# Routing stage reordered on TensorE, and the first expert's tokens gathered directly in turned form

## What is computed

```
x = x + mix @ w_out
h = rmsnorm(x, ln_ffn_g)
logits = h @ w_router + b_router
top_val, top_idx = lax.top_k(logits, 4)
probs = softmax(top_val)
for each expert e:                      # 32 of them, 3 matrices of 1024x1024 each
    xb = rows of h whose top_idx holds e
    g = min(xb @ w_gate[e] + b_gate[e], 7);  u = clip(xb @ w_up[e] + b_up[e], -7, 7)
    a = g * sigmoid(1.702 * g) * (u + 1)
    y[those rows] += probs * (a @ w_down[e] + b_down[e])
x = x + y;  return rmsnorm(x, ln_final_g)
```

## Time and profile before

| | |
|---|---|
| median of three runs | 1139.98 us (1139.12 to 1140.4) |
| span of the profiled execution, first to last instruction | 1137.4 us |
| around the span (median less span) | 2.6 us |
| TensorE busy | 1092.5 us, 96% of the span |
| ScalarE / VectorE busy | 200.9 / 316.3 us |
| DMA | 439.24 MB, mean 386 GB/s |

### The profile page before, as it was taken

One profiled execution on the slowest core, in us unless ns is written; L12 is line 12 of the kernel. 1 busy time (PEld: TensorE's weight loads), 2 busy tenths in 40 slices (PEclk: granted clock), 3 DMA queues, 4 the chain that ended last, 5 costly groups with the idle time before them and its releaser, 6 DMA issues.

```text
span 1137.4 us, 12484 instructions
## 1 busy us (share of the span) xinstructions
PE 1092.5 (96%) x5391; PEld 494.9 (44%) x5391; DVE 316.3 (28%) x686; ACT 200.9 (18%) x350; POOL 3.6 (0%) x11
## 2 busy tenths in 40 slices
PE   7999999999999999999999999999999999999996
PEld 6888889733343333333333333333333333333332
DVE  7566778421111111111111111111111111111121
ACT  5345556210000000000000000001110000000011
POOL 0000000000000000000000000000000000000000
PEclk9999999999999999999999999999999999999999
DMA  9854229999999999999999999999999999999996
GB/s 351 269 175 159 110 77 405 414 403 414 427 429 426 429 426 429 428 428 429 428 429 428 429 427 429 428 428 429 429 428 428 429 428 429 429 429 428 426 427 256
DMA packets 46280, 439.24 MB, mean 386 GB/s; under 512 B 4106, under 2 KB 5666, under 8 KB 20900
## 3 DMA queue, kind: packets, MB, share of 16 engines
q1 hardware_dynamic: 46084, 438.48, 92.5%
q10 hardware_dynamic: 160, 0.27, 0.1%
HBM read 437.68 MB, written 1.05 MB: 386 GB/s over the span
## 4 chain that ended last, share of the span: by engine, by line
PE 80%; DMA 15%; DVE 2%; ACT 2%; issue 1%; SPq 0%; POOL 0%; DVEq 0%; POOLq 0%
PE ps L1075 49%; PE ps L722 5%; PE ps L1099 4%; DMA attn<-in_w_gate_dram 4%; PE ps L1004 4%; DMA attn<-in_w_up_dram 4%; DMA pool<-in_w_up_dram 4%; DMA pool<-in_w_down_dram 3%; PE ps L752 2%; PE ps L802 2%; PE ps L760 2%; PE ps L1052 1%; ACT o_t L656 1%; PE ps L855 1%; PE ps L857 1%; PE ps L856 1%
## 5 line engine op out<-in xcount | busy, mean ns | idle before, releaser
L1075 PE MATMUL ps<-pool,o_t 128*64 128x512 f32 x2144 | 482.6, 597 | 16.9 <-ACT o_t L656 12.1
L1075 PEld LDWEIGHTS ps<-pool,o_t 128*64 128x64 f32 x2144 | 148.6, 137 | 307.0 <-issue 282.7
L1545 DVE TENSOR_SCALAR v_tok<-ps 128x512 f32<-128x512 f32 x32 | 22.1, 692 | 497.7 <-PE ps L1075 497.7
L656 ACT ACTIVATE o_t<-ps 128x512 f32<-128x512 f32 x32 | 19.1, 597 | 323.1 <-PE ps L722 323.1
L1075 PE MATMUL ps<-slot_gt,o_t 128*64 128x512 f32 x304 | 69.4, 598 | 5.4 <-ACT o_t L656 4.1
L1075 PE MATMUL ps<-slot_wv,o_t 128*64 128x512 f32 x304 | 69.4, 598 | 4.1 <-ACT o_t L656 4.1
L1075 PE MATMUL ps<-attn,o_t 128*64 128x512 f32 x320 | 72.2, 593 | 1.1 <-DMA attn<-in_w_gate_dram 0.9
L643 ACT ACTIVATE attn<-v_tok 128x512 f32<-128x512 f32 x32 | 20.2, 630 | 247.4 <-DVE v_tok L1545 247.4
L1099 PE MATMUL ps<-attn,o_t 64*128 64x512 f32 x256 | 63.6, 615 | 0.0
L1004 PE MATMUL ps<-xs,work 128*64 128x512 f32 x256 | 60.7, 593 | 0.0
L722 PEld LDWEIGHTS ps<-cst,work 128*128 128x128 f32 (+1 forms) x294 | 35.8, 170 | 54.8 <-issue 52.1
(11 more groups left out here) (195 smaller groups left out, 952.7 us busy)
## 6 DMA issues: line engine op xcount, KB each, us to landing
pool<-in_w_gate_dram SPq DMA_DIRECT2D x44, 2048.0 KB, 27.1
pool<-in_w_up_dram SPq DMA_DIRECT2D x43, 2048.0 KB, 26.6
pool<-in_w_down_dram SPq DMA_DIRECT2D x41, 2048.0 KB, 25.9
attn<-in_w_gate_dram SPq DMA_DIRECT2D x7, 2048.0 KB, 26.3
slot_wv<-in_w_up_dram SPq DMA_DIRECT2D x7, 2048.0 KB, 23.5
slot_gt<-in_w_down_dram SPq DMA_DIRECT2D x7, 2048.0 KB, 32.0
slot_gt<-in_w_up_dram SPq DMA_DIRECT2D x6, 2048.0 KB, 21.3
slot_gt<-in_w_gate_dram SPq DMA_DIRECT2D x6, 2048.0 KB, 25.6
```

What stands on the lines that cost most here:

```text
L656: act.activation(dst.rearrange("p (h j) c -> p j h c", h=2), ps[:, G, :].rearrange("p (j h c) -> p j h c", h=2, c=SLOTS), ACT.Copy)\
L1075: mm = pe.matmul(ps[SLOTS * h:SLOTS * h + SLOTS, bank, :], lhs[:, k, :], ring[(at + j) % RING][:, r, 512 * h:512 * h + 512], start=(k == 0 ...
```

## The change

1. ACT copies the transposed half (1, 0) before it squares half (1, 1); TensorE makes the transpose of (1, 0) ahead of the first logits and not behind them.
2. For expert 0 alone, `gather_block`, the copy by ACT and `turn_gathered(0)` are replaced by `first_gather(b, h)`: four matmuls with 128 columns of `xs` (every fourth) as the stationary operand and `sel` (64 columns) as the moving one. Their output has the model columns on the partitions and the slots along the row, which is the turned form. Half 0 goes to bank X, half 1 to bank Y + 3; DVE takes each with a semaphore of its own (`first_half`, `xg_turned`).
3. All five `keep_busy` matmuls go. `residual_in(0, 0)` moves behind the place matmul of block 1, `residual_in(0, 1)` behind expert 2; so `combine` now starts three output banks rather than two.

```
--- before.py
+++ after.py
@@ -236,6 +236,7 @@
 
         ps = ctx.enter_context(nc.psum_tensor("ps", [P, 8, 512], F32))
         G, U, X, DN, Y = 0, 1, 2, 3, 4
+        FIRST_X = (X, Y + 3)
         PROJ = ((0, 1), (4, 5))
         MIX = (0, 1, 6, 7)
         PV = 7
@@ -293,7 +294,7 @@
             sem("count_done"), sem("nov_ready"), sem("ostart_done"), sem("tab_ready"), sem("tab_done"), sem("over_ready"))
         pieces_used = sem("pieces_used")
         pick_ready = sem("pick_ready")
-        first_sel = sem("first_sel")
+        first_sel, first_half = sem("first_sel"), sem("first_half")
         sel_ready, gathered, x_rows_ready = sem("sel_ready"), sem("gathered"), sem("x_rows_ready")
         xg_turned, xg_half, xg_ready = sem("xg_turned"), sem("xg_half"), sem("xg_ready")
         g_ready, sig_done, act_ready = sem("g_ready"), sem("sig_done"), sem("act_ready")
@@ -629,8 +630,8 @@
             square_residual(0, 1)
             turned_residual(0, 1)
             square_residual(1, 0)
+            turned_residual(1, 0)
             square_residual(1, 1)
-            turned_residual(1, 0)
             turned_residual(1, 1)
 
             for b in range(NB):
@@ -647,7 +648,7 @@
                 act.activation(dst, ps[:, bank, 0:SEQ], ACT.Copy).then_inc(sel_t_ready, 1)
 
             def gathered_out(n):
-                act.wait_ge(gathered, n + 1)
+                act.wait_ge(gathered, n)
                 act.activation(x_rows, ps[:, X, :], ACT.Copy).then_inc(x_rows_ready, 1)
 
             def turned_activation(n, dst=a_t):
@@ -687,7 +688,6 @@
                 act.wait_ge(pieces_used, FIRST[LAST + 1, 2] + 2)
                 act.activation(y_bufs[1][0:SLOTS], ps[0:SLOTS, U, :], ACT.Copy).then_inc(y_ready, 1)
 
-            gathered_out(0)
             for n in range(LAST):
                 expert(n)
             last_pair()
@@ -988,11 +988,10 @@
             pe.wait_ge(w_rt_ready, 1)
             pe.wait_ge(bias_hi_ready, 2)
             pe.wait_ge(bias_lo_ready, 1)
+            turn_residual(1, 0)
             logits_of(0, 0)
             logits_of(0, 1)
-            turn_residual(1, 0)
             turn_residual(1, 1)
-            residual_in(0, 0, start=True)
             logits_of(1, 0)
             pe.wait_ge(chosen_ready, 1)
             pe.matmul(ps[:, DN, 0:E], tri_far, chosen[:, 0, :], start=True, stop=True).then_inc(pos0_done, 1)
@@ -1021,13 +1020,21 @@
                     pe.matmul(ps[:, Y + 2 * b + q // 2, at:at + SEQ], prob_t[:, P * b:P * b + P], b_dn[q],
                               start=False, stop=False, skip_group_check=True)
 
+            def first_gather(b, h):
+
+                for j in range(4):
+                    at = SLOTS * j
+                    mm = pe.matmul(ps[:, FIRST_X[h], at:at + SLOTS], every_fourth(xs[:, b, 512 * h:512 * h + 512], j), sel[:, b, :],
+                                   start=(b == 0 and j == 0), stop=(b == NB - 1), skip_group_check=True)
+                return mm
+
             pe.matmul(ps[:, G, E:2 * E], ones, chosen[:, 0, :], start=True, stop=False)
             pe.wait_ge(first_sel, 1)
-            gather_block(0)
-            residual_in(0, 1, start=True)
+            first_gather(0, 0)
+            first_gather(0, 1)
             pe.wait_ge(chosen_ready, 2)
             pe.matmul(ps[:, G, E:2 * E], tri_far, chosen[:, 1, :], start=False, stop=True).then_inc(pos_done, 1)
-            keep_busy(2)
+            residual_in(0, 0, start=True)
 
             def turn_rows(bank, rows_ap):
                 for j in range(4):
@@ -1035,7 +1042,7 @@
                 return mm
 
             def turn_gathered(n):
-                pe.wait_ge(x_rows_ready, n + 1)
+                pe.wait_ge(x_rows_ready, n)
                 turn_rows(X, x_rows).then_inc(xg_turned, 1)
 
             def turn_activation(n):
@@ -1097,17 +1104,15 @@
                     for h in range(2):
                         rows_of = slice(SLOTS * h, SLOTS * h + SLOTS)
                         mm = pe.matmul(ps[:, Y + 2 * b + h, :], sel_ts[last][rows_of, P * b:P * b + P], y_bufs[last][rows_of, :],
-                                       start=(first and b == 1), stop=False, skip_group_check=True)
+                                       start=(first and (b, h) != (0, 0)), stop=False, skip_group_check=True)
                         mm.then_inc(combined, 1)
 
             pe.wait_ge(first_sel, 2)
-            gather_block(1)
+            first_gather(1, 0).then_inc(first_half, 1)
+            first_gather(1, 1).then_inc(xg_turned, 1)
             for b in range(NB):
                 mm = pe.matmul(ps[0:E, U, 0:1], chosen[:, b, :], ones[:, 0:1], start=(b == 0), stop=(b == NB - 1))
             mm.then_inc(count_done, 1)
-            keep_busy(2)
-            turn_gathered(0)
-            keep_busy(1)
 
             def second_turned():
                 turn_gathered(1)
@@ -1155,6 +1160,8 @@
                     if first and i == 4:
                         residual_in(1, 0)
                         residual_in(1, 1)
+                    if first and i == 2:
+                        residual_in(0, 1)
 
             def landed_once(rounds):
                 return 16 * (rounds + 1)
@@ -1553,10 +1560,10 @@
                 dve.wait_ge(g_step, n + 1)
                 dve.scalar_tensor_tensor(a_rows, u_act, 1.0, g_act, ALU.add, ALU.mult).then_inc(act_ready, 1)
 
-            dve.wait_ge(xg_turned, 1)
-            for h in range(2):
+            for h, turned in enumerate((first_half, xg_turned)):
+                dve.wait_ge(turned, 1)
                 dve.tensor_tensor(x_g[:, 4 * h:4 * h + 4, :],
-                                  ps[:, X, :].rearrange("p (j h c) -> p j h c", h=2, c=SLOTS)[:, :, h, :],
+                                  ps[:, FIRST_X[h], 0:4 * SLOTS].rearrange("p (j c) -> p j c", c=SLOTS),
                                   gain[:, :, h, :], ALU.mult).then_inc(xg_ready if h else xg_half, 1)
             weigh(0)
             weigh(1)
```

19 lines of the change are left out of this document (8 added, 11 removed).

## The result

The changed kernel takes 1146.09 us (median of 5 runs, 1145.13 to 1147.39) against 1139.98 before: 6.1 us more, a ratio of 1.0059 with a 95% interval of 1.0049 to 1.007. It is slower, by 0.6%. The forecast was 1139.8 us, no change that can be measured, in a range that ended at 1141.9. The profiled execution took 1147.39 us, with a span of 1145.5.

The account below looks back on a forecast made before the run. The weight stream was taken as the bound; slower gathers nearly ate the gains of the shorter tail (1.3 us) and earlier logits (0.33). Span 1137.4 - 0.2 = 1137.2, with 2.6 around it 1139.8 us; range 1139.0 to 1141.9.

Parts of the forecast that it names:

- The bound: Whole kernel: the weight stream sets the end; its hole at 224 to 232 us, 1.1 or 2.3 us, follows first product.
- the rival by which the start doesn't matter: Low DMA window at 224 to 232 us comes from small parts, not idle time: 1140.0 us, chance 0.08.
- The order: Routing stage, transposes of (1, 0) first: logits (1, 1) done 0.33 us sooner, block 0's table half a microsecond later.
- The tail from the last gather to the first product: End of routing stage: only count 0.22 and bias matmul 0.42 remain, where 1.96 us lay before.
- 0.13 per gather instruction: Direct gather for expert 0: 32 strided instructions at 0.13 us each, 2.08 us for each block.
- The upper bound of 0.178: Direct gather with strided loads paid in full: 0.178 us each, first product 1.3 us later, 1141.3 us, chance 0.10.
- The rule of the Trainium skill: Gather's strided weights: crossing to a new 16-byte line pays a penalty, so 212 against 140 ns would count in full.
- the mechanism as a rival: Clock falls in the narrow stretch before the first product: one fall 1141.4 us, chance 0.25; two 1143.0, chance 0.10.
- one or two losses of 1.6 us: Clock's price: one fall costs 1.6 - 0.2 = 1.4 us; paid over gathers and first product, 3.2 - 0.2 = 3.0 us.
- frees nothing more: Routing stage: the keep_busy matmuls stood in waits the chain had anyway, so removing them gains no further time.
- the forecast's 0.2 us sooner: Sum for the changed stage: first product starts at 224.34 against 224.52, making the whole 0.2 us shorter.
- a reason for a fall from the new order alone: Four more transposes in front, not counted as busy for the clock, bring a fall nearer; time of one fall.

Follow-up runs that it names:

- experiment 10: experiment 4 with a 512-column keep_busy matmul ahead of each of the sixteen strided gather matmuls: 1144.97 us, ratio 1.0042 to the kernel before.
- experiment 5: The changed kernel with first_gather taking 128 neighbouring columns of xs, not every fourth (expert 0's output differs): 1144.67 us, ratio 1.0046 to the kernel before.
- experiment 12: One more execution of Experiment 6's kernel, unchanged, for a profile: 1137.56 us.
- experiment 2: The changed kernel with the old gather, copy and transposes put back; residuals stay moved, keep_busy stays out: 1140.79 us, ratio 1.0012 to the kernel before.
- experiment 4: experiment 3 with residual_in(0, 1) between the two blocks' gathers in place of behind expert 2: 1144.86 us, ratio 1.005 to the kernel before.
- Experiment 6: experiment 4 with contiguous gather columns, expert 0's first four weight pieces and the gain reordered to match: median 1142.45 us in two groups, ratio 1.001 to before.
- experiment 3: The changed kernel with residual_in(0, 0) back between the transposes of (1, 1) and the logits of (1, 0): 1146.38 us, ratio 1.006 to the kernel before.
- Experiment 1: The kernel before with only the new order of transposes, logits, copy and square: 1139.42 us, ratio 0.9998.
- experiment 7: experiment 2 with two keep_busy matmuls ahead of the logits of (1, 0), writing bank Y + 1: 1140.13 us, ratio 1.0002 to the kernel before.
- experiment 8: Experiment 6 with one keep_busy behind logits (1, 0), logits (1, 1) and between halves of block 0's gather: 1139.0 us, ratio 0.999 to the kernel before.
- 9: Experiment 6 with two keep_busy matmuls at each of the three places used in experiment 8: 1139.41 us, ratio 0.9997 to the kernel before.

## Why the prediction was wrong

**The bound was right.** The end is set by the weight stream, whose only hole is at 224 to 232 us and whose depth follows the first product. The added DMA idle time of the profile (6.2 us) comes close to the added time of the medians (6.1), and experiment 10 has as much from a later start at full clock. This answers the rival by which the start doesn't matter. `residual_in(0, 1)` behind expert 2 cost nothing: at 300 to 320 us the share is 1.01.

**The order was right.** Measured from the stage's start, experiment 5 has logits (1, 1) done after 5.13 us where the earlier trace rows give 5.52: 0.39 sooner, forecast 0.33. The table for block 0 came 0.47 later in the changed kernel, forecast 0.5. The tail from the last gather to the first product was 0.64 in experiment 12 (223.32 to 223.96), as forecast, in place of 1.96.

**The first step that failed: 0.13 per gather instruction.** It was taken from the strided transposes, eight of which took 1.11 against 1.02, with the argument that loads overlap and most of the stride's cost is hidden. The upper bound of 0.178 added the transposes' 72 ns to the logits' pace. Both were wrong. The load of the gather's own form took 330 ns, and 192 contiguous, so the stride costs 138 ns and not 72. Loads do overlap with what runs beside them, since the pace is shorter than a load in both forms; but it went from 0.111 to 0.238 per instruction, so 127 of the 138 ns show. The forecast had 4.16 us for 32 instructions; they took 3.77 + 3.58 = 7.35, which is 3.2 us more, and even the upper bound allowed only 5.7. The error was to take the nearest row by its access pattern, though the matmul under the load was another: a transpose streams 128 columns, a gather instruction 64. That this is why the transposes hid their stride is likely, but no run isolates it.

The rule of the Trainium skill that the prediction set against its sum (SBUF — State Buffer, section Door 1: The DMA port swizzle: an access that crosses to a new 16-byte line pays a penalty) was the better guide. This case agrees with it: by the page's size every fourth float32 column is a new line each time, and the load goes from 192 to 330 ns. No run here had a stride between one and four columns, so the line's size itself isn't shown.

**The second: the clock.** The prediction had the mechanism as a rival, read from the earlier trace rows, with a chance of 0.35 in both forms, and priced it as one or two losses of 1.6 us. It happened: all five runs have a mean clock of 0.989 to 0.991 against 0.995 and above in before, and in the profile it lasted 17 us. Its price on the chain, each row against its like at full clock: L997, L963 and L1031 +1.4, L1036 and the residual L970 +1.2, count and bias +0.4, together 3.0 us ahead of the first product, and 1.6 in it. The form of the rival was right and its size wrong: a loss of 1.6 was the loss of one product, while here most of a stage ran at half clock as well. The falls were 3.4 us long at 339 us, some 10 in experiments 2, 4, 5 and 6, 13.6 in experiment 3 and 17 in the changed kernel. The longest two are those with the strided gather and at most one wide matmul ahead of its end; that the slow gather is what stretches them is argued from this, not shown.

**The sentence that carried this** was that removing the `keep_busy` matmuls "frees nothing more". The sum gave them no part in holding the clock; only the rival named them. The sentence isn't quite right of the chain either. Between the logits and the end of the gathers the old kernel had a residual of 1.05 us and two `keep_busy` of together 0.55, the new order has one residual of 0.86 in their place, and the forecast's 0.2 us sooner needs the 0.7 us that this gives: its stated reasons alone (2.14 more for the gathers, 1.3 and 0.33 less) would make the start 0.5 us later. Experiment 1 keeps them and the residuals, and the clock; experiment 2 drops them and loses it in three of ten runs; experiment 7 puts two in at the residual's old place and loses it in none. The other wide matmuls seem to count alike: with the residuals back at one and at two places the fall came at 220 and at 221.7 in place of 217, one profile each.

The Trainium skill, TensorE: Matmul & The Clock Gate, Part 4, says that transposes don't count as busy for the clock the way other matmuls do. The prediction saw in this a reason for a fall from the new order alone; experiment 1 has that order, and ten runs kept their clock. Whether transposes count is not shown by it, as the wide matmuls stood there too.

**How the sum adds up.** Forecast 11.3 us from the stage's start to the first product; 3.2 for the gather and 3.0 for the clock make 17.5; measured 17.2, where the kernel before has 11.5. With 1.6 inside the product its end is 7.4 us later than before, and SP's first issue behind it 6.6 (19.2 after the stage's start against 12.6), which is close to the 6.2 us of DMA idle time.

**What stays open.** What decides, from one execution of experiment 2 or 6 to the next, whether the clock falls: the instructions are the same. Experiment 12 also had no fall behind 334 us, where the old kernel shows one, and nothing here says why. The best version tried is that of experiment 8, 0.999 [0.9981, 0.9999]: a gain of 0.1% whose interval only just leaves out 1, one of many such comparisons, so it isn't certain. Experiment 6 with the clock held is 1.4 to 2.8 us faster than before, but held it in 5 of 11 executions. That is more than its 0.56 us of earlier start explains; the rest wasn't isolated.

## What to carry to other kernels

Price a weight load by its own form (dtype, columns, stride) under the matmul it feeds: behind short matmuls a slow load shows nearly in full, and a row of the same access pattern under another matmul doesn't bound it. Before removing matmuls that "do nothing", or the wide ones from a stretch of narrow ones, price the clock over everything up to the next dense stretch, as a loss that may come in some executions only; several runs, with the mean clock of each, show it where one profile may not. And where a stream feeds the kernel, find the one event on which it hangs: here a single start time carried two unrelated causes to the end at roughly one microsecond for one.

## What the runs showed of the hardware

- A float32 weight load of 128 columns on 128 partitions: 192 ns contiguous (experiment 12), 310 to 332 ns with every fourth column (experiment 4), at full clock. At half clock the contiguous one takes 333 (median of the second gather of experiment 5), the strided one stays at 329 to 337 in the changed kernel. Sixteen gather instructions: contiguous 1.73 to 1.81 at full clock, 3.31 at half; strided 3.81 and 3.58.
- The clock fell while TensorE was never without work: in experiment 4 it was busy in all of 213 to 224 us, and the clock fell at 221.7.
- With a few more 512-column matmuls among the narrow ones (experiments 7, 8 and 9) no profile has a fall in this stage, and none of the 31 executions has the time or the mean clock of one (at most 1141.39 us, 0.995 and above). The mean clock alone doesn't settle a run: the profile of experiment 8 has 0.995, from a fall at 339 to 345.7 us, where the stream is full. One such matmul took 0.28 to 0.31 us there, two 0.46 to 0.54.
- The same kernel can hold or lose the clock from execution to execution: held in 5 and lost in 6 of the 11 of experiments 6 and 12, worth 5.2 to 5.5 us. One execution of each kind was profiled; the others are told by their times and mean clocks.
